# One plain gate and up pair instead of two, with two block products of the next pair between the turned rows

## The reference

```python
h = rms_norm(x, pre_ffn_g[l])
gu = jnp.einsum('bsd,df->bsf', h, w_gate_up[l])
gate, up = gu[..., :FFN_HIDDEN], gu[..., FFN_HIDDEN:]     # FFN_HIDDEN = 2816
y = jnp.einsum('bsf,fd->bsd', jax.nn.silu(gate) * up, w_down[l])
x = x + rms_norm(y, post_ffn_g[l])
```

## Time and profile before

| | |
|---|---|
| median of 3 runs | 1085.18 us (1084.9 to 3580.0) |
| the profiled execution's own time | 1084.86 us |
| its span | 1082.7 us |
| mean granted TensorE clock | 0.999 |
| PE busy | 1074.8 us, 99% |
| PEld busy | 965.0 us, 89% |
| DVE busy | 608.6 us, 56% |
| ACT busy | 589.5 us, 54% |
| POOL busy | 568.1 us, 52% |

### The profile page before, as it was taken

The page is one execution under the profiler, slowest core; times in us unless marked ns, Lnnn a source line. Parts: engine busy times, 40 slices in busy tenths (PEclk is TensorE's granted clock), DMA queues, the critical chain, the costliest instruction groups (busy, mean ns, idle before and its releaser), DMA issues.

```text
span 1082.7 us, 17501 instructions
## 1 busy us (share of the span) xinstructions
PE 1074.8 (99%) x6788; PEld 965.0 (89%) x6788; DVE 608.6 (56%) x1011; ACT 589.5 (54%) x1151; POOL 568.1 (52%) x442
## 2 busy tenths in 40 slices
PE   9999999999999999999999999999999999999997
PEld 7888788999999999888888888889999999988886
DVE  4376554878888884010344756457888888820103
ACT  6767784755555554221457568656655555531212
POOL 3534364467666665544344344634766666654440
PEclk9999999999999999999999999999999999999999
DMA  8423212424433434523353222232343343363212
GB/s 291 147 60 104 71 59 81 153 79 118 117 100 97 118 103 169 176 97 97 87 161 103 78 79 78 75 126 87 103 117 100 96 117 107 91 218 119 98 51 78
DMA packets 145335, 119.37 MB, mean 110 GB/s; under 512 B 3802, under 2 KB 120036, under 8 KB 145252
## 3 DMA queue, kind: packets, MB, share of 16 engines
q1 hardware_dynamic: 145236, 118.24, 35.1%
q10 hardware_dynamic: 16, 0.00, 0.0%
HBM read 111.94 MB, written 6.29 MB: 109 GB/s over the span
## 4 chain that ended last, share of the span: by engine, by line
PE 99%; ACT 0%; DMA 0%; DVE 0%; issue 0%; DVEq 0%; ACTq 0%
PE banks L595 30%; PE banks L597 30%; PE banks L596 30%; PE banks L660 2%; PE banks L688 2%; PE banks L604 1%; PE banks L673 1%; PE banks L865 1%; PE banks L699 1%; DMA x_rows<-in_x_dram 0%; PE banks L706 0%; ACT junk L1080 0%; PE banks L950 0%; DVE scratch L1509 0%; DVE x_rows L1543 0%
## 5 line engine op out<-in xcount | busy, mean ns | idle before, releaser
L534 POOL TENSOR_TENSOR w_lo<-raw,w_hi 128x512 fp32r<-128x512 f32 x204 | 264.7, 1321 | 312.2 <-ACT w_hi L1072 312.2
L552 POOL TENSOR_TENSOR w_lo<-raw,w_hi 128x512 fp32r<-128x512 f32 x200 | 260.8, 1314 | 146.6 <-ACT w_hi L1141 142.1
L595 PE MATMUL banks<-xg_hi,w_hi 128*128 128x256 f32 (+1 forms) x880 | 273.5, 311 | 0.0
L597 PE MATMUL banks<-xg_lo,w_hi 128*128 128x256 f32 (+1 forms) x880 | 271.3, 308 | 0.0
L596 PE MATMUL banks<-xg_hi,w_lo 128*128 128x256 f32 (+1 forms) x880 | 271.2, 308 | 0.0
L1072 ACT ACTIVATE w_hi<-raw 128x1024 fp32r<-128x1024 f32 x102 | 107.2, 1061 | 161.4 <-PE banks L597 146.9
L1141 ACT ACTIVATE w_hi<-raw 128x512 fp32r<-128x512 f32 x200 | 125.1, 630 | 114.9 <-DVE raw L1794 61.1
L597 PEld LDWEIGHTS banks<-xg_lo,w_hi 128*128 128x128 f32 x880 | 168.0, 191 | 8.4
L595 PEld LDWEIGHTS banks<-xg_hi,w_hi 128*128 128x128 f32 x880 | 168.1, 191 | 8.3
L596 PEld LDWEIGHTS banks<-xg_hi,w_lo 128*128 128x128 f32 x880 | 168.1, 191 | 7.5
L595 PE MATMUL banks<-w_hi,hid_hi 128*128 128x512 f32 x352 | 137.2, 390 | 0.0
(11 more groups left out here) (180 smaller groups left out, 1875.8 us busy)
## 6 DMA issues: line engine op xcount, KB each, us to landing
raw<-in_w_gate_up_dram SPq DMA_DIRECT2D x88, 512.0 KB, 4.1
raw<-in_w_down_dram SPq DMA_DIRECT2D x44, 512.0 KB, 3.8
raw<-in_w_in_dram SPq DMA_DIRECT2D x40, 512.0 KB, 3.8
raw<-in_w_out_dram SPq DMA_DIRECT2D x16, 512.0 KB, 3.7
x_spill<-x_rows SPq DMA_DIRECT2D x8, 512.0 KB, 4.3
x_rows<-x_spill SPq DMA_DIRECT2D x8, 512.0 KB, 4.9
x_rows<-in_x_dram SPq DMA_DIRECT2D x4, 512.0 KB, 7.4
out_dram<-x_rows SPq DMA_DIRECT2D x8, 256.0 KB, 2.1
```

What stands on the lines that cost most here:

```text
L534: last = tt(lo[:, piece], raw_half(l, c, h)[:, piece], hi[:, piece].bitcast(F32), ALU.subtract)
L552: tt(lo, full, hi.bitcast(F32), ALU.subtract).then_inc(w_ready, 1)
L595: mm(o, stat[0], mov[0], start=first, stop=False)
L597: return mm(o, stat[0], mov[1], start=False, stop=last)
```

## The change

F0 becomes 1, so pair 1 is a block pair too. Its first two products, B11 and B21, stand where half of its plain gate tile stood, between the transposes of row block 3 and the right halves of pair 0 (`first_blocks`); its other five follow the right halves (`rest_of_first_blocks`). DVE makes the sums T1 and T3 of this pair before it norms row block 3, and T1's low part between the two halves' low parts of row blocks 2 and 3. The S sums are made in another order, in other PSUM banks. ACT loads the silu table after the boundary by a silu of one column. POOL makes the low part of B11, B21 and T3 of pair 1 before that of S3.

```diff
-    F0 = 2
+    F0 = 1
+    FIRST_T_BANKS = {T1: 5, T2: 0}
...
-                for c in range(C_GU + 1, C_GU + F0):
-                    for h in range(2):
-                        low(l, c, h)
+                for i in (B11, B21, T3):
+                    factor_low(l, F0, i)
                 s3_low(l, 0)
                 s3_low(l, 1)
-                for f in range(F0, FT):
+                for i in (T4, B22):
+                    factor_low(l, F0, i)
+                for f in range(F0 + 1, FT):
...
+            def first_blocks(l):
+
+                b0 = SETS[F0 % 2][0]
+                pe.wait_ge(x_kept_ready, 4 * l + 3)
+                block_product(l, F0, B11, "A11", b0, right, first_blocks_done)
+                block_product(l, F0, B21, "A12", b0, left, first_blocks_done)
+
+            def rest_of_first_blocks(l):
+                b0, b1, b2 = SETS[F0 % 2]
+
+                pe.wait_ge(s_ready, 4 * l + 2)
+                block_product(l, F0, T1, "S1", b1, right, n_done=3)
+                pe.wait_ge(s3_ready, 2 * (l + 1))
+                block_product(l, F0, T3, "S3", b1, left)
+                block_product(l, F0, T4, "A22", b2, right)
+                pe.wait_ge(m1_copied, t_upto(l, F0, 0, 1))
+                pe.wait_ge(s_ready, 4 * (l + 1))
+                block_product(l, F0, T2, "S2", b0, right)
+                pe.wait_ge(s4_ready, 2 * (l + 1))
+                block_product(l, F0, B22, "S4", b2, left)
...
                 turn_rows(group, 3)
-                pe.wait_ge(x_kept_ready, 4 * l + 3)
-                gate_up(l, 1, 0, left, False)
+                first_blocks(l)
                 pe.wait_ge(xg_ready, 8 * group + 8)
                 gate_up(l, 0, 0, right)
                 gate_up(l, 0, 1, right)
-                gate_up(l, 1, 0, right)
-                pe.wait_ge(x_kept_ready, 4 * l + 4)
-                gate_up(l, 1, 1)
-                for f in range(F0, FT):
+                rest_of_first_blocks(l)
+                for f in range(F0 + 1, FT):
                     gate_up_blocks(l, f)
...
+                def first_sums(r):
+                    if r == ST - 1:
+                        t_sum(F0, T1)
+                        t_sum(F0, T3)
+
+                boundary(2 * l, (first_sums, lambda: t_low(F0, T1)))
```

## The result

The changed kernel takes 1087.93 us (median of 9 runs, 1087.84 to 1088.11), the kernel before 1085.01 us (median of 9, lowest 1084.90): 2.9 us or 0.27% more, ratio 1.0027 with a 95% interval of 1.0017 to 1.0037. Forecast were 1088.3 us, in a range of 1085.2 to 1090.4. One of the runs of before took 3580.0 us; the ratio leaves it out. The profiled execution of the changed kernel took 1088.08 us.

The account below looks back on a forecast made before the run. PE was taken as the bound, busy 1074.8 of 1082.7 us. Its 1.13 us saving a layer was outweighed by late feeders: +1.57 a layer, +3.1 in both, 1088.0 on the profiled 1084.86, plus 0.32: 1088.3 us, range 1085.2 to 1090.4.

Parts of the forecast that it names:

- PE saves 1.13 us a layer: PE from the transposes to B21 of pair 3: 15.92 us of work instead of 17.05, 2.3 us in both layers.
- Rival 3: Sums T1 and T3 ahead of row block 3's norm meet POOL's work, transposes late: +3.2 us, 1091.5 us; chance 0.08.
- the walk: Step along DVE's new list, with ACT and POOL, timing each operation in layer 1 against when PE wants it.
- First shortage: PE at B22 of pair 1: wanted at 753.23, ready at 754.07, 0.84 us late plus 0.08 for a start from rest.
- rule of turns: DVE and POOL alternate on shared SBUF reads, ends 0.55 us apart for DVE and 1.16 for POOL.
- The total of 1.3 at B21 of pair 2: PE waits for ACT's copy_m1(2) before B21 of pair 2, due at 757.55: 1.3 us late in all.
- Second shortage: PE at B21 of pair 3 waits for ACT's copy_m1, starts at 770.34 instead of 767.63: 2.7 us late in all.
- the 2.18 us of idle: DVE's idle time ahead of the turn before copy_m1; said to be the slack before, used up by the change.
- Recovery of 1.95 a pair: Behind pair 3, DVE's turn takes 8.13 us against PE's 10.08, regaining 1.95 a pair; no more is lost.
- The sum: B21 of pair 3 comes 1.57 us later a layer, +3.1 in both, giving 1088.3 us against 1085.18.
- list of signs: Expected marks: PE waits on w_lo and m, some 5.4 us; no DVE idle before pair 2's T1 sum beyond handovers.
- Rival 1: Most of DVE's added work is hidden in idle time, only the saving stays: 1082.9 us; chance 0.12.

Follow-up runs that it names:

- kernel of 1082.87 us: Changed kernel with high parts of S4 and B22 early, sums of u of pairs 1 to 3 and their ACT copies moved forward: 1082.87 us, ratio 0.9980.
- copy-early run: Changed kernel with silu_11(2) and copy_m1(3) on ACT ahead of the high parts of B22 of pair 3 and B11 of pair 4: 1085.95 us, ratio 1.0008.
- three added operations: Kernel before with the low part of S2's second half made four times, three more DVE operations a layer: 1085.07 us, ratio 1.0000.
- S4's high parts early: Changed kernel with the high parts of S4 and of B22 of pair 1 ahead of hidden_high(0) on ACT: 1085.78 us, ratio 1.0006.
- the same edit: B11 and B21 of pair 1 put behind pair 0's right halves: 1088.13 us in the changed kernel, 1086.34 us in the kernel of 1082.87 us.
- the run with B22's high part left behind: Changed kernel with S4's high parts ahead of hidden_high(0) on ACT, but B22's behind it: 1085.78 us, ratio 1.0007.
- pair 1's move: Pair 1's sums of u ahead of pair 2's T2 sum on DVE, against the 1083.71 us kernel (S4 highs and pair 3's copy early): 1084.02 us.

## Why the prediction held, point by point

- **PE saves 1.13 us a layer: right.** Nowhere in the changed kernel can it be seen by itself, since other waits lie over it. The kernel of 1082.87 us shows it: 2.19 us below the kernel before, for 2.26 foretold, and 0.95 a layer in the trace with 0.19 lost before T4 of pair 2. The Trainium skill (TensorE: Matmul & The Clock Gate, Back-to-back issue gap) gives the 109 ns that the prediction set beside the row's 0.12 for a single matmul, and says itself that a stream goes by other figures; an estimate by it for the 240 matmuls from 738.19 to 767.25 is 26.2 us. The trace has 29.06, and the row's distance decides.
- **T1 and T3 ahead of row block 3: nothing, as foretold.** The idle time of 1.54 us fell to 0.21, which is 1.54 less the two sums' 1.33. Rival 3 needed 0.5 us of overlap with POOL; POOL's low part ended at 736.38, 0.08 behind the start of the first sum, both sums ran 0.69 and nothing was late.
- **The S sums 0.10 later: right.** From the transposes' end they start at +1.79 (742.45 less 740.66); the walk had 1.78.
- **First shortage, 0.84 and 0.08 at B22 of pair 1: right.** The start was 0.95 late, and the slow distance behind it (756.08 to 756.27) cost 0.07: 1.02 against 0.92. The T1 sum took 1.17 and the T3 sum 1.66, the two prices of the rule of turns (1.19 and 1.71 in the walk).
- **The total of 1.3 at B21 of pair 2: right in size, wrong for the most part in the waiter.** I had PE wait for ACT's `copy_m1(2)` there. It waited 0.20 before, at B11 of pair 2, for POOL, and then found the copy all but made: it ended at 760.71, and B21 started at 760.76, 0.15 behind the matmul before it (0.03 too much, with a slow distance of 0.22 behind) and 1.31 later than with nothing late (20.10 from 740.66, against 18.79). The walk had POOL's B11 low part end at 755.73 and never compared this with PE's arrival behind the late B22 (754.15 + 1.44 = 755.59): by its own numbers it was 0.14 late there.
- **Second shortage at B21 of pair 3: right, and nearly exact.** DVE's low part of T2 of pair 2 starts at +21.82, foretold +21.80. From there to the end of `copy_m1(3)` the trace has 9.65 (762.48 to 772.13), the very 9.65 that was read from the turn before. PE's B21 came at +31.53, foretold +31.50, and the slow distance behind it cost 0.10, foretold 0.08; late by 2.65 against 28.88 with nothing late, and by 2.75 with that distance, foretold 2.7. The copy-early run adds what the prediction did not say: 1.0 us of it was ACT's order, not DVE's work.
- **That the 2.18 us of idle were the slack, and the change has used it up: only in part.** At the same point of the list DVE still idles 1.18 us after the change (762.48), while ACT makes the high parts of T4 and T2, so 1.00 of the 2.18 was used up here. The 2.16 us of the three added operations went into two other waits, of 0.99 and 1.64 us, which do not stand in the new list.
- **Recovery of 1.95 a pair, no later waits: right.** No wait behind pair 3. The next pair's low part of T2 waited 1.18 for ACT again, at 778.60, less than the 2.18 of before.
- **The sum.** +1.62 a layer, slow distance included, for +1.57; 1087.93 for 1088.3. What was added up is 0.1 too small in both layers, and the total still came out 0.4 too high. 0.17 of that is the median of the kernel before that it was added to (1085.18, of nine runs 1085.01). The rest is scatter: the profiled execution after, at 1088.08, lies 0.15 above its own median, that before, at 1084.86, 0.15 below.
- **In the list of signs**, "5.4 us of waits in all" was counted from start to start with the slow distances, and by that count it is 5.5; without those distances it is 4.8, and the list of waits, which counts from modelled ends, has 3.8. The sign "no idle time of DVE before its T1 sum of pair 2 beyond handovers" did not come: the 1.18 us at 753.50 stand there, and so they did in the walk (next point).
- **Rival 1** fell, but one sentence against it was false: "no idle time of DVE is left between 740.5 and 756". The walk itself had DVE end `hidden(0)` at 750.40 and the second S4 low part, after 1.27 of work, at 752.86, so it held 1.19 us of idle time, and the trace shows 1.18 at 753.50. Taking that idle time away (S4's high parts early) gave part of rival 1's time; POOL took its place.

What the prediction did not ask is whether the chain had to be this long. Orders of the same work that are 4 to 5 us shorter existed; that says nothing against the forecast, which was about the order in the diff.

Not tried: moving PE's wait for the copy of `m` from before B21 to before T2, which would give DVE's chain more room without touching ACT. PE could then write one half of a bank while ACT still reads the other half, and no run here shows what comes of that. So it is open what the kernel gains where PE's order gives way instead of ACT's and DVE's. Nor was the first wait split between POOL's own 1.30 us and the turns it takes with DVE.

## What to carry to other kernels

Where one engine bounds a kernel and never waits, taking work from it gives time only as long as the engines that feed it still arrive. Walk their queues, in order, from the point where the change puts more on them to the point where their slack has paid it back, and compare each product with the new and earlier time of the bound engine. Before moving a filler, look at what it covers: two DVE operations were free in the 1.18 us in which DVE waited for ACT, and put ahead of that wait they cost the kernel 1.5 us (1085.53 against 1084.02), until two others filled the hole. And take a fill's worth only from a kernel in which nothing behind it is late: here the same edit was worth 0.2 or 3.5 us.

## What the runs showed of the hardware

- **Two DVE sums of which the second needs the first lie 0.72 us apart, independent ones 0.60.** In the changed kernel T2's sum at 758.71 is followed by a sum of `u` at 759.30 and its dependent one at 760.01 (0.71), and T4's sum follows that at 760.62. Put side by side, T2's and T4's sums (766.96 and 767.68 above) are 0.72 apart. An order that alternates two chains saves 0.12 us a time; pair 1's move broke one such place and cost about that in each layer.
- **DVE and POOL take turns where a DVE operation has both inputs in SBUF.** Two low parts of S4 took 1.28 us with POOL idle (the run with B22's high part left behind) and 2.39 beside two of POOL's low parts; a T sum took 0.69, 1.17 or 1.66. The operations of DVE with one input in PSUM stayed at 0.68 or 0.69 beside the same work of POOL. The Trainium skill (SBUF — State Buffer, Who interferes with whom) says that a DVE instruction with two SBUF inputs contends with a GpSimd instruction that reads SBUF, and one with at most one SBUF input, outside the 2-port modes, does not; the trace agrees. What was not expected is that moving such an operation out of its idle time (S4's high parts early) saved nothing by itself, since it moved under POOL's.
